# Two attention sequences in one fp32 kernel: VectorE's logits moved to the front of each beat, ScalarE's normalisation moved one beat later

## The reference

```python
def forgetting_attention(q, k, v, log_f):          # first block, 8 heads of 64
    ...
        s = jnp.einsum('bqhd,bkhd->bhqk', qb, kb).astype(jnp.float32) * scale
        s = s + c[:, :, q0:q1, None] - c[:, :, None, :q1]
        s = jnp.where(valid, s, -jnp.inf)
        p = jax.nn.softmax(s, axis=-1)
        outs.append(jnp.einsum('bhqk,bkhd->bqhd', p.astype(vb.dtype), vb))
...
def chunked_relpos_attention(q, k, v, rel_bias):   # second block, 8 heads of 64
    ...
    s = s + bias[None, None]
    s = jnp.where(valid[None, :, None, None, :], s, NEG_INF)
    p = jax.nn.softmax(s, axis=-1)
    out = jnp.einsum('bnhqk,bnkhd->bnqhd', p.astype(v.dtype), v_band)
```

## Time and profile before

| | before |
|---|---|
| median of 3 runs | 1009.93 us (1009.12 to 1011.12) |
| profiled execution, its own time | 1012.43 us |
| its span, first to last instruction | 1010.6 us |
| TensorE matmul busy | 980.9 us (97% of the span) |
| TensorE idle (span less busy) | 29.7 us |
| VectorE busy | 657.3 us (65%) |
| ScalarE busy | 485.5 us (48%) |
| GpSimd busy | 70.5 us (7%) |
| granted TensorE clock, mean | 0.995 |

### The profile page before, as it was taken

The page is one execution under the profiler, slowest core; times in us unless marked ns, Lnnn a source line. Parts: engine busy times, 40 slices in busy tenths (PEclk is TensorE's granted clock), DMA queues, the critical chain, the costliest instruction groups (busy, mean ns, idle before and its releaser), DMA issues.

```text
span 1010.6 us, 13022 instructions
## 1 busy us (share of the span) xinstructions
PE 980.9 (97%) x4784; PEld 817.1 (81%) x4784; DVE 657.3 (65%) x1203; ACT 485.5 (48%) x963; POOL 70.5 (7%) x158
## 2 busy tenths in 40 slices
PE   8999999999999999999889999899999999999998
PEld 7888988788888888777778778788888888888886
DVE  6487878859787768467577776877444454445453
ACT  6458687743223445589685654334124223323420
POOL 4001001011112011000000000110000000000000
PEclk9999999999999999999999999999999999999999
DMA  7104221257789415342433225337413223322221
GB/s 294 75 25 178 67 103 53 84 197 291 286 289 331 174 56 153 114 125 78 136 94 115 63 63 207 127 103 131 163 56 112 84 86 123 107 102 84 84 73 52
DMA packets 34080, 129.81 MB, mean 128 GB/s; under 512 B 8905, under 2 KB 8905, under 8 KB 24418
## 3 DMA queue, kind: packets, MB, share of 16 engines
q1 hardware_dynamic: 23538, 98.27, 29.0%
q0 software_dynamic: 7408, 26.75, 7.6%
q10 hardware_dynamic: 3072, 3.98, 1.1%
HBM read 119.45 MB, written 5.27 MB: 123 GB/s over the span
## 4 chain that ended last, share of the span: by engine, by line
PE 78%; DVE 12%; ACT 4%; issue 3%; DMA 2%; SPq 0%; POOL 0%; ACTq 0%; DVEq 0%; POOLq 0%
PE psum L1842 23%; PE psum L1844 23%; PE psum L1843 23%; PE psum L2009 2%; DVE wl L1081 2%; PE psum L1988 2%; PE psum L2038 1%; PE psum L2041 1%; DMA raw<-in_wall 1%; DVE two L1620 1%; DVE ptl L1293 1%; DVE p_sb L1282 1%; DMA value_rows<-rows 1%; DVE hl L1121 1%; DVE tmp L1599 1%
## 5 line engine op out<-in xcount | busy, mean ns | idle before, releaser
L1842 PE MATMUL psum<-hh,wh 128*128 128x512 f32 (+1 forms) x720 | 277.2, 385 | 0.7 <-DVE hl L1121 0.6
L1844 PE MATMUL psum<-hh,wl 128*128 128x512 f32 (+1 forms) x720 | 268.5, 373 | 0.0
L1843 PE MATMUL psum<-hl,wh 128*128 128x512 f32 (+1 forms) x720 | 268.2, 373 | 0.0
L582 ACT ACTIVATE wh<-raw 128x512 fp32r<-128x512 f32 x292 | 169.5, 620 | 134.9 <-PE psum L1844 118.9
L1081 DVE TENSOR_TENSOR wl<-raw,wh 128x512 fp32r<-128x512 f32 x292 | 192.5, 684 | 18.1 <-ACT wh L582 17.6
L1844 PEld LDWEIGHTS psum<-hh,wl 128*128 128x128 f32 x720 | 135.6, 188 | 24.1
L1842 PEld LDWEIGHTS psum<-hh,wh 128*128 128x128 f32 x720 | 135.8, 189 | 22.8 <-DVE hl L1121 1.6
L1843 PEld LDWEIGHTS psum<-hl,wh 128*128 128x128 f32 x720 | 136.0, 189 | 19.1 <-issue 0.7
L1842 PE MATMUL psum<-wh,ah 128*128 128x512 f32 x320 | 125.8, 393 | 0.0
L1844 PE MATMUL psum<-wh,al 128*128 128x512 f32 x320 | 124.6, 389 | 0.0
L1843 PE MATMUL psum<-wl,ah 128*128 128x512 f32 x320 | 124.6, 389 | 0.0
(11 more groups left out here) (282 smaller groups left out, 1468.0 us busy)
## 6 DMA issues: line engine op xcount, KB each, us to landing
raw<-in_wall SPq DMA_DIRECT2D x75, 1024.0 KB, 5.0
wa<-in_wada POOLq DMA_DIRECT2D x20, 512.0 KB, 5.9
gt<-in_wada POOLq DMA_DIRECT2D x20, 512.0 KB, 7.1
wb<-in_wada POOLq DMA_DIRECT2D x8, 512.0 KB, 7.3
xt<-in_xcols SPq DMA_DIRECT2D x8, 264.0 KB, 8.4
cb<-c_rows SPq DMA_DIRECT2D x8, 264.0 KB, 3.5
x<-in_x SPq DMA_DIRECT2D x4, 512.0 KB, 8.1
x_kept<-x SPq DMA_DIRECT2D x4, 512.0 KB, 2.8
```

Of the source, the lines that this page charges most:

```text
L582: e.activation(home(w)[0][:, 512 * c:512 * c + 512], raw_of(w, c), ACT.Copy).then_inc(a["wh"], 1)
L1842: e.matmul(out_, lh, rh, start=start, stop=False, skip_group_check=True)
L1843: e.matmul(out_, lh, rl, start=False, stop=False, skip_group_check=True)
L1844: return e.matmul(out_, ll, rh, start=False, stop=stop, skip_group_check=True)
```

## The change

Two edits. On ScalarE, `normalize` has age 6 instead of 5: it comes one beat later. On VectorE, `logits` is the first operation that is looked up in a beat instead of the last. No operation is added or removed, and TensorE's list stays the same.

```diff
-AGE = dict(logits=1, max=2, exp=3, rcp=4, norm=5, sig=1, scan=2, ph=1, pl=2, half=1, both=2, oh=3, ol=4,
+AGE = dict(logits=1, max=2, exp=3, rcp=4, norm=6, sig=1, scan=2, ph=1, pl=2, half=1, both=2, oh=3, ol=4,
            gate=3, oh_fg=4, ol_fg=5)
...
                 def at(age):
                     return flat[b_ - age] if b_ >= age else None
 
+                if (x_ := at(AGE["logits"])) and x_[0] == "S" and x_[1] not in SB:
+                    logits(*x_[1:])
                 if ends(x_ := at(AGE["ol_fg"])) and x_[1] in FG and x_[1] % 2:
                     out_lower(x_[1])
...
                 if ends(x_ := at(AGE["both"])):
                     both_out(x_[1])
-                if (x_ := at(AGE["logits"])) and x_[0] == "S" and x_[1] not in SB:
-                    logits(*x_[1:])
```

## The result

| | before | after |
|---|---|---|
| median | 1009.64 us (8 runs, 1009.12 to 1011.98) | 1006.41 us (8 runs, 1004.11 to 1008.06) |
| ratio, 95% interval | | 0.9963 (0.995 to 0.9976) |
| profiled execution, its span | 1012.43, 1010.6 us | 1008.06, 1006.2 us |
| TensorE busy in the profile | 980.9 us | 978.6 us |
| granted clock, mean | 0.995 | 0.996 |

Faster by 0.37% by the ratio. The forecast was 1.4 us; the medians differ by 3.2 us, or 3.5 from the median of three runs that the forecast started from, and the two profiled executions by 4.4. The profiled execution of before is one of its slow-clocked ones: its mean granted clock is 0.995, as in 20 of the 74 other runs of this kernel on record, so the difference of the profiles is larger than that of the medians.

A forecast was written before the change was run, and what follows sets the result against it. TensorE was busy for 980.9 of 1010.6 us, so order could win only inside 29.7 us of idle time. Terms -0.9 - 0.3 + 0.2 + 0.5 - 0.9 = -1.4 on 1009.93 gave 1008.5 us, range 1006.2 to 1011.6.

The forecast's parts named there:

- S(5,2), -0.9: First block: logits of S(5,3) take the gate L1306's slot, so S(5,2) waits less than 1.57 us; -0.9 us.
- S(1,2), -0.3: First block, S(1,2) to T(0,1): logits start earlier, but a normalisation moves behind the key copies; T(0,1) 0.25 earlier, booked -0.3 us.
- the small waits, +0.2: First block: T waits where its `ptl` copy had too little to spare; one place, head 2's meta transpose, +0.2 us.
- a sign that it was wrong: Any of three: `ptl` waits growing over 2 us, a T waiting for L720, or VectorE setting the end at T(15,1).
- The mask, 0: GpSimd's mask, for which L1268 waited 7.9 us: VectorE gets up to that back, TensorE gains nothing; 0 booked.
- Heads 8 to 12, +0.2: Second block before T(13,1): delayed `ptl` copies nearly cancel against ScalarE's earlier start; net +0.3 up to T(10,1), head 11 cancelling.
- T(13,1), +0.3: T(13,1), waiting 2.63 us: L745 starts some 0.4 sooner, but logits of 0.75 stand before the copy; +0.3 us.
- T(15,1), -0.9: T(15,1), waiting 2.58 us: one normalisation moves behind L745, which starts about 1.2 us earlier; -0.9, between nothing and -1.2.
- the third sign: Waits of transposes for `ptl` growing by more than 2 us in all would show the prediction wrong.
- The clock: Rival: T(15,1)'s stall falls to 1.4 to 1.7 us and 1.8 us of clock loss returns; -3.2, 1006.7 us, chance 0.25.
- its second rival: Heads 8 to 13: `ptl` delays behind logits are not absorbed; +1.5, or +3.3 (1013.2 us) with clock loss; chance 0.15.

The follow-up runs named there:

- the best version: Kernel before with normalisation at age 6 in heads 8 to 15 and logits first in heads 1 and 5 only: 1003.97 us, ratio 0.9938.
- Head 15 alone: Kernel before with normalisation at age 6 for head 15 only, logits left last: 1007.56 us, ratio 0.9979.
- the added maxima: Normalisation at age 6 everywhere, logits last, plus two, four or eight useless VectorE maxima before T(15,1)'s `ptl` copy: 1005.94, 1005.93, 1008.06 us.

## Why the prediction was off

**S(5,2), -0.9:** right. 1.57 became 0.69, by the slot that the forecast named: the gate L1306 is now behind the logits.

**S(1,2), -0.3, and the small waits, +0.2:** wrong in sum. S(1,2) did shrink, 1.30 to 0.95, but T(0,1) started 0.06 us late instead of 0.25 early. The step took the normalisation of 272 columns out from ahead of the key copies and had them start at 93.3. But the normalisation of 400 columns ahead of it has moved one place back too and fills the room: the key copies began at 93.80, no earlier than before, the normalisation ended at 95.45, and T(0,1) waited for it.

T(0,3) waits for its probabilities as well, which had been ready with next to nothing to spare (0.29 us on the weight load above; with normalise later alone its matmul waits 0.37). The prediction named a T that waits for L720 as a sign that it was wrong; there are two.

Of the small waits the meta transpose of head 2, which was named, does not wait; T(2,0) does, 0.32 us, though its copy had 1.0 us to spare. The copy came 1.55 us later, at 127.21 instead of 125.66, because the logits ahead of it first waited 0.88 us for their scores; the rest is the 0.63 us of the next logits, which now stand ahead of it. The sum counted a logits operation moved to the front by its length alone, and never by this wait. T(2,0) starts 0.7 us late in all, so the first block ended 0.4 us ahead instead of 1.0.

**The mask, 0:** right in its size. VectorE won 6.7 us of waiting there, and its logits' new waits for scores took 3.1 of it back in the first block and 5.2 in the second. The prediction had the gate L1306 alone as what holds up the mask, in three places; by the trace it is `wl` copies and L1311 as well, in ten places in all, and the `ptl` copy leaves the mask alone, as it said.

**Heads 8 to 12, +0.2:** this is the step that failed on the side of the order. (The prediction writes +0.3 up to T(10,1), +0.3 for T(13,1) and +0.5 together; the last two leave +0.2 here, and the first says +0.3.) Single waits changed as forecast: T(8,0) grew by 0.50, 0.75 being the worst case, and L2271's wait of 0.61 vanished. But I let ScalarE's head start and VectorE's delay cancel at each place, and counted T(10,1) as a loss that stays. From the start of head 8's transposes to that of head 11's the profile after gained 0.9 us: 0.3 up to T(10,1), and 0.6 behind it, of which 0.5 are a wait that the sum does not have, that of L1842 for the `qk` of L1557 (0.84 us before, 0.35 after).

Normalise later without logits first gained 0.8, logits first alone 0.5: either move alone wins here, and together they win hardly more, because the waits that logits first lengthens are taken back at the next wait for queries and keys: that of L1842 is 0.84 us in the best version's profile and 0.35 with logits first added in heads 8 to 15, that of L2271 0.13 and nothing. That ScalarE's L959 and L929 come forward with each exp that goes ahead of a normalisation is how I read the first 0.8; L2271's wait shows it for one place, 0.61 us before and 0.14 with normalise later alone. (With logits first alone it is gone as well, because TensorE comes there later.) No experiment took it apart further.

**Before head 8, no term:** from the start of T(7,1) to S(8,3) another 0.7 us were won, 0.64 of it in the wait of S(8,3) for its keys' lower part, a DMA (1.15 us before, 0.51 after). It is 0.50 to 0.53 in all eleven profiles with late normalisation in heads 8 to 14 and 0.75 to 1.15 in the three without, though no normalisation of those heads comes before it. What goes with it is in the traces: in the three profiles with the longer wait, and in no other, a packet of queue 14, whose kind is "instruction", started 1.9 to 2.1 us after the first of the two transfers of `low` was issued and before the second had landed; in the other eleven the next such packet came 6.8 us after it or later. The second transfer took 2.6 to 3.0 us to land in the three and 2.35 to 2.37 in the eleven. The row from the window 427 to 431 us of before, which the window 426 to 430 of after does not have (queue, packets, MB, share):

```profile
q14 instruction: 1, 0.01, 1.0%
```

So these 0.6 us are probably the loading of code, whose place in time the edit shifts, and not the order of operations. No experiment tested it. Head 15 alone has the longer wait, 0.75, so 0.2 us of what heads 8 to 14 seem to give above it are of this kind.

**T(13,1), +0.3:** right in the pair of profiles, 2.63 to 2.94. By the profiles of the experiments it is about -0.6 for normalise later and +0.8 for logits first, 0.3 of the latter through rows that came later. But the step took this wait as fixed. It depends on when rows come back from DRAM: VectorE waited 1.4 and 1.3 us for them in the profiles of logits first alone and of head 15 alone, where T(13,1) waited 0.26 and 0.22, and 3.4 us or more in the others.

**T(15,1), -0.9:** right, 2.58 to 1.79. L745 starts 2.62 us earlier than before, 0.9 more than T(13,1) does, where 1.2 was expected. VectorE is busy without a gap from L1576 at 522.32 to the `ptl` copy, so it now sets this end: the bound of the step (VectorE late by itself) is real, but it bites only after 0.8 us are won. The prediction had named this, too, as a sign that it was wrong. Its size held all the same, since 0.8 lies inside the bounds that the step gave; the third sign, waits for `ptl` that grow by more than 2 us, did not come (0.7).

**The clock:** put as a rival with 0.25, for the very reason that made it come true. "Against it: nothing shows where between 1.57 and 2.58 the fall begins": it begins between 1.97 and 2.35 here, and the forecast stall of 1.4 to 1.8 lay clear of it. That could not be read from the rows of before alone. With 1.6 us in place of its 1.8, the rival's mechanism is confirmed by the trace and by the added maxima. Its other half, that the longer T(13,1) would lose as much, did not weigh: that place loses its clock before and after.

So of the profile's 4.4 us 1.6 are clock at T(15,1), 0.8 its shorter stall, 0.9 heads 8 to 12, 0.7 the piece before head 8, 0.4 the first block, less 0.3 at T(13,1); 0.3 lie outside the attentions.

The order at T(15,1) was right. What failed is the term for heads 8 to 12 (+0.2 forecast, -0.9 measured), which kept a lengthened wait on the books that the next wait gives back; the clock, left at nothing in the likeliest case (-1.6 measured); and the nothing before head 8 (-0.7 measured). The first block erred the other way (-1.0 forecast, -0.4 measured). That the rival's 1006.7 us lies near the measured 1006.41 is in part luck: it has the clock of the two profiles right, but its order part is the same -1.4, and the medians, unlike the two profiles, hold only some 1.1 us of clock (below). The upper end of the range, 1011.6, does not follow from the prediction's own figures: the middle of its second rival, +1.5 to +3.3 on 1009.93, is 1012.3. Nothing hangs on it here.

## What to carry to other kernels

When a move delays one helper's piece and brings another's forward, price it up to the next point where TensorE waits for anything of either, not stall by stall: in heads 8 to 11 both lengthened stalls were given back there. An operation moved to the front of an in-order queue brings its own wait with it: price how long it will stand for its input, not only how long it runs. A reordering for all heads is worth splitting: here each edit was a gain in some heads and none or a cost in others, and the version that uses each only where a stall asked for it has the lowest median, though its lead over normalise later in heads 8 to 15 alone is within the scatter of the medians. A stall near the point where the clock falls is worth more than its length, here 1.6 us more; where a change takes a long stall under one whose clock held, make the clock part of the forecast and not a rival.

## What the runs showed of the hardware

- The clock falls behind a stall, and not by its length alone. T(7,1) waits 1.92 or 1.93 us in all fourteen profiles; the stretch from 200 to 220 us shows 1.00 in eight and 0.91 or 0.92 in six, before and after among these. T(13,1) kept the clock with 2.79 us in one profile and lost it with 1.99 in another. Only T(15,1) was clear-cut. What else decides stays open.
- The clock goes with most of the scatter. Of 74 runs of the kernel before, the 20 with a mean granted clock of 0.995 took 1011.3 us in the mean, the 38 with 0.996 or 0.997 took 1009.6, the 12 with 0.998 took 1008.1 and the 4 with 1.000 took 1006.7. The granted clock is 0.9965 in the mean over these 74 and 0.9976 over after's eight; by that (0.0011 of 1008 us) some 1.1 us of the difference between the medians are clock. This is an estimate and not measured apart.
- A maximum over 128x128 took 0.27 us on VectorE, near the 0.28 that had been expected from the wider ones; in a row of several they start 0.20 us apart, so that two took 0.46 us, four 0.85 and eight 1.62.
- GpSimd's mask of 128x128 took 0.29 us alone or beside a `ptl` copy, which has one input in PSUM, and 0.60 to 0.62 beside VectorE operations with both inputs in SBUF.
- The second transfer of `low` for head 8, from SBUF to SBUF (128 KB), landed 2.35 to 2.37 us after its issue in eleven profiles, and 2.6 to 3.0 in the three in which a packet of queue 14, of the kind "instruction", fell into it.
